# Routing rearranged, norm chain with squares from PSUM, and four modulation pairs as plain fp32 products in a two-layer decoder step

## What is computed

```python
def run_layer(x, c, s0, l):
    mod = (jax.nn.silu(c) @ w_ada[l] + b_ada[l])[:, None, :]
    sh1, sc1, g1, sh2, sc2, g2 = jnp.split(mod, 6, axis=-1)
    h = _rmsnorm(x, norm_pre_mix[l]) * (1.0 + sc1) + sh1
    mix, s_new, v_rows = _mixer(h, s0, lb[l], ...)          # gMLP and HGRN2 branches, then w_out
    x = x + g1 * _rmsnorm(mix, norm_post_mix[l])
    h = _rmsnorm(x, norm_pre_ffn[l]) * (1.0 + sc2) + sh2
    f = _swiglu(h, ...) if l % 2 == 0 else _moe(h, ...)
    return x + g2 * _rmsnorm(f, norm_post_ffn[l]), s_new, v_rows

def _moe(h, w_router, b_router, w_gate, w_up, w_down):
    logits = (h @ w_router) + b_router
    top_vals, top_idx = lax.top_k(logits, TOP_K)            # 2 of 8
    combine = ...                                           # softmax of the two, per expert
    for e in range(N_EXPERTS):
        out = out + combine[..., e:e + 1] * _swiglu(h, w_gate[e], w_up[e], w_down[e])   # 1024 -> 2816 -> 1024
```

## Time and profile before

| | before |
|---|---|
| median of 3 runs | 2442.24 us (2438.5 to 2442.84) |
| profiled execution | 2435.61 us |
| its span | 2433.8 us |
| mean granted TensorE clock | 0.958 |
| TensorE busy | 2254.9 us, 93% |
| VectorE busy | 1656.9 us, 68% |
| ScalarE busy | 1261.8 us, 52% |
| GpSimd busy | 73.6 us, 3% |

### The profile page before, as it was taken

One profiled execution on the slowest core, in us unless ns is written; L12 is line 12 of the kernel. 1 busy time (PEld: TensorE's weight loads), 2 busy tenths in 40 slices (PEclk: granted clock), 3 DMA queues, 4 the chain that ended last, 5 costly groups with the idle time before them and its releaser, 6 DMA issues.

```text
span 2433.8 us, 36240 instructions
## 1 busy us (share of the span) xinstructions
PE 2254.9 (93%) x13683; PEld 2040.0 (84%) x13683; DVE 1656.9 (68%) x1771; ACT 1261.8 (52%) x1267; POOL 73.6 (3%) x111
## 2 busy tenths in 40 slices
PE   5999999997999979999989759999999999999996
PEld 4899898986999969999989648888888888788884
DVE  5566566576555564655656368888888888888886
ACT  5433235354544444223434336766767677676764
POOL 3000000101000010000010000000000000000000
PEclk9999999998999989999989759999999999999997
DMA  8444345554566634232444209988989989898993
GB/s 266 151 126 152 104 148 156 191 178 121 177 196 191 199 112 139 83 105 96 139 147 139 104 25 328 348 331 310 343 298 359 333 321 352 297 346 320 348 334 135
DMA packets 279077, 520.13 MB, mean 214 GB/s; under 512 B 17911, under 2 KB 191049, under 8 KB 278962
## 3 DMA queue, kind: packets, MB, share of 16 engines
q1 hardware_dynamic: 270656, 493.94, 58.6%
q0 software_dynamic: 7936, 23.24, 3.0%
q10 hardware_dynamic: 370, 1.35, 0.2%
HBM read 507.19 MB, written 11.27 MB: 213 GB/s over the span
## 4 chain that ended last, share of the span: by engine, by line
PE 77%; DVE 9%; DMA 6%; issue 4%; ACT 3%; SPq 0%; DVEq 0%; ACTq 0%; POOL 0%; POOLq 0%
PE ps L1542 10%; PE ps L1543 9%; PE ps L1574 8%; PE ps L1917 5%; PE ps L1923 5%; PE ps L1918 5%; DMA mraw<-in_w_exp_up 5%; PE ps L1593 4%; PE ps L1954 4%; PE ps L1955 4%; PE ps L1960 4%; PE ps L1663 3%; PE ps L1886 2%; PE ps L1502 2%; DVE rstd L516 2%
## 5 line engine op out<-in xcount | busy, mean ns | idle before, releaser
L1015 DVE TENSOR_TENSOR mlo<-mraw,mhi 128x2048 fp32r<-128x2048 f32 (+1 forms) x319 | 691.5, 2168 | 85.1 <-ACT mhi L1340 73.8
L1340 ACT ACTIVATE mhi<-mraw 128x2048 fp32r<-128x2048 f32 (+1 forms) x320 | 582.8, 1822 | 275.0 <-DMA mraw<-in_w_exp_up 213.1
L473 DVE TENSOR_TENSOR wlo<-raw,whi 128x1024 fp32r<-128x1024 f32 x340 | 414.4, 1219 | 298.6 <-ACT whi L1102 275.9
L1542 PE MATMUL ps<-h1h,whi 128*128 128x320 f32 x1248 | 402.0, 333 | 25.5 <-DVE h1l L547 20.0
L1102 ACT ACTIVATE whi<-raw 128x1024 fp32r<-128x1024 f32 x340 | 338.8, 1046 | 108.0 <-PE ps L1599 75.1
L1543 PE MATMUL ps<-h1l,whi 128*128 128x320 f32 x1248 | 378.1, 314 | 0.0
L1917 PE MATMUL ps<-mhi,xeh 128*128 128x512 f32 (+1 forms) x864 | 327.7, 379 | 7.2 <-DVE sg L1032 4.7
L1918 PE MATMUL ps<-mhi,xel 128*128 128x512 f32 (+1 forms) x864 | 322.5, 373 | 0.0
L1542 PEld LDWEIGHTS ps<-h1h,whi 128*128 128x128 f32 x1248 | 241.4, 193 | 33.2 <-issue 29.4
L1543 PEld LDWEIGHTS ps<-h1l,whi 128*128 128x128 f32 x1248 | 241.8, 194 | 2.6 <-issue 2.6
L1923 PE MATMUL ps<-mlo,xeh 128*128 128x512 f32 (+1 forms) x864 | 225.7, 373 | 0.3 <-DVE mlo L1015 0.3
(11 more groups left out here) (327 smaller groups left out, 3175.1 us busy)
## 6 DMA issues: line engine op xcount, KB each, us to landing
mraw<-in_w_exp_down SPq DMA_DIRECT2D x198, 512.0 KB, 6.4
mraw<-in_w_exp_gate SPq DMA_DIRECT2D x154, 512.0 KB, 4.7
mraw<-in_w_exp_up SPq DMA_DIRECT2D x144, 512.0 KB, 5.9
raw<-in_w_in SPq DMA_DIRECT2D x128, 512.0 KB, 3.8
raw<-in_w_ada SPq DMA_DIRECT2D x96, 512.0 KB, 3.6
mraw<-in_w_exp_gate SPq DMA_DIRECT2D x72, 384.0 KB, 3.6
mraw<-in_w_exp_up SPq DMA_DIRECT2D x72, 384.0 KB, 4.8
raw<-in_w_ffn_gate SPq DMA_DIRECT2D x22, 512.0 KB, 5.5
```

The lines of the kernel that those rows point to most:

```text
L473: V.tensor_tensor(WLO[:, (u - 1) % RAW_UNITS, 0:w], RAW[:, u % RAW_UNITS, 0:w], WHI[:, u % HI_UNITS, 0:w].bitcast(F32), ALU.subtract).then ...
L1015: V.tensor_tensor(MLO[:, (n - 1) % RAW_RING, 0:w], MRAW[:, n % RAW_RING, 0:w], MHI[:, n % HI_RING, 0:w].bitcast(F32), ALU.subtract).then_i ...
L1340: A.activation(MHI[:, n % HI_RING, 0:w], MRAW[:, n % RAW_RING, 0:w], ACT.Copy).then_inc(m_hi, 1)
L1542: M.matmul(out_, w, v[0], start=start, stop=False, skip_group_check=True)
```

## The change

- **Start.** The sequence of pairs is scale 4 to 7, then shift 0 to 3 (FIRST_PAIRS). Units 8 to 15, which hold the four shift pairs, aren't split: TensorE multiplies `raw` with an fp32 copy of the conditioning vector (CSF, nine columns). Each pair is turned by itself one pair behind. x is normalized and scaled while the shifts are computed; the lower bounds' softmax stands behind the operands. One transfer of GpSimd (the masks) is issued later.
- **Norms.** ScalarE squares the PSUM banks, then copies. Statistics of the chunk before stand in the middle of a chunk. VectorE multiplies each chunk with the gate while the projection runs; behind the reciprocal it takes two d at a time with all 320 columns (640 elements): one product and one sum. The samples' share of the pre-norm is done in halves of four d, its first step ahead of the statistics; low parts of coming units (`lows`) stand inside the wait for them. The first chunk behind a norm goes d by d (BY_K).
- **Routing.** Two units of sample transposes and two of the prompt stand ahead of the router, two behind it. Memsets move to GpSimd. The first two expert pairs are split ahead of the router's result, the next on both engines ahead of the gathers. `choose(0)` follows the positions. Count and extra tables move into job 0, which is written out ahead of the loop, behind positions 17, 19, 21, 23, 25 and 28 (TABLE_PAIRS).
- **End.** Transposes in two halves of four d, copies shared by ScalarE and VectorE.

```diff
+HM_ORDER = [4, 5, 0, 2, 1, 3]
+TABLE_PAIRS = {17: 0, 19: 1, 21: 2, 23: 3, 25: 4, 28: 5}
...
+FIRST_PAIRS = (4, 5, 6, 7, 0, 1, 2, 3)
+DIRECT = range(8, 16)
...
+            def gate_dve(l, w, g):
+                dve.wait_ge(ada_made, (g + KD) // 2)
                 st(V.tensor_tensor(AM[:, :, :], MOD[:, g:g + KD, :],
                                    VEC[:, 1, w + 8 * l:w + 8 * l + 8].unsqueeze(2).broadcast_to([P, KD, SEQS]),
                                    ALU.mult))
+            def gated(d):
+                return see.note(V.tensor_scalar(SA[:, d, 0:TP], SA[:, d, 0:TP], AM[:, d, 0:1], None, ALU.mult), dve_step)
+            def gated_chunk(c, k):
+                dve.wait_ge(psum_out, c + 1)
+                gated(2 * k)
+                gated(2 * k + 1)
+            def post_norm_dve():
+                st(V.tensor_tensor(samples(SA), samples(SA), seq(AM), ALU.mult))
                 stats_dve(T, D, KD)
-                st(V.tensor_tensor(SA[:, :, TP:T], SA[:, :, TP:T], rb_samples, ALU.mult))
-                st(V.tensor_tensor(samples(SA), samples(SA), seq(AM), ALU.mult))
-                V.tensor_tensor(X[:, :, TP:T], X[:, :, TP:T], SA[:, :, TP:T], ALU.add)
                 made = []
-                for d in range(KD + 1):
-                    if d < KD:
-                        made.append(see.note(V.scalar_tensor_tensor(SA[:, d, 0:TP], SA[:, d, 0:TP], AM[:, d, 0:1], rb,
-                                                                    ALU.mult, ALU.mult), dve_step))
-                    if d:
-                        dve.wait_ge(dve_step, made[d - 1])
-                        see.note(V.tensor_tensor(X[:, d - 1, 0:TP], X[:, d - 1, 0:TP], SA[:, d - 1, 0:TP], ALU.add),
-                                 x_ready)
+                for q in range(5):
+                    s, p = slice(2 * q, 2 * q + 2), slice(2 * q - 2, 2 * q)
+                    if q < 4:
+                        made.append(see.note(V.tensor_tensor(SA[:, s, :], SA[:, s, :], over_k(RSTD[:, 0:T], 2),
+                                                             ALU.mult), dve_step))
+                    if q:
+                        dve.wait_ge(dve_step, made[q - 1])
+                        V.tensor_tensor(X[:, p, :], X[:, p, :], SA[:, p, :], ALU.add).then_inc(x_ready, 2)
+                        see.n[id(x_ready)] = see.n.get(id(x_ready), 0) + 2
...
+            def first_modulation(i):
+                see.next(turned)
+                modulation(FIRST_PAIRS[i], 1,
+                           PS[:, 4 + i % 2, 0:32].rearrange("p (t n) -> p t n", t=2)[:, :, 0:SEQS])
+                dve.wait_ge(ada_made, i + 1)
+            lo_until(6)
+            first_modulation(0)
+            lo_until(8)
+            first_modulation(1)
+            stats_dve(T, D, KD)
+            first_modulation(2)
+            first_modulation(3)
+            st(V.scalar_tensor_tensor(AM[:, :, :], MOD[:, KD:2 * KD, :], 1.0,
+                                      VEC[:, 1, 0:KD].unsqueeze(2).broadcast_to([P, KD, SEQS]), ALU.add, ALU.mult))
+            st(V.tensor_tensor(samples(HT), samples(X), seq(AM), ALU.mult))
+            st(V.tensor_tensor(HT[:, :, TP:T], HT[:, :, TP:T],
+                               RSTD[:, TP:T].unsqueeze(1).broadcast_to([P, KD, TS]), ALU.mult))
+            for d in range(KD):
+                see.note(V.scalar_tensor_tensor(HT[:, d, 0:TP], X[:, d, 0:TP], AM[:, d, 0:1], RSTD[:, 0:TP],
+                                                ALU.mult, ALU.mult), sem("xr_made"))
+            dve.wait_ge(sem("xr_made"), KD)
...
+            mark["hm"] = x[0]
+            def hm_low(i):
+                aux()
+                dst, src = hm_unit(HML, HM_ORDER[i], x[0] - 1)
+                see.next(sem("hm_hi"))
+                V.tensor_tensor(dst, src, hm_unit(HMH, HM_ORDER[i], 0)[0].bitcast(F32), ALU.subtract)\
+                    .then_inc(aux_out, 1)
+            for i in range(4):
+                hm_low(i)
+            st(V.memset(LG[:, :, :], 0.0))
+            m_lo_part(0, 0)
+            m_lo_part(0, 1)
...
+            choose(0)
+            m_lo_part(0, 2)
+            m_lo_part(0, 3)
+            dve.wait_ge(m_aux_out, 2)
+            V.memset(SW[:, :], 0.0).then_inc(y_made, 1)
+            def tables(part):
+                if part == 0:
+                    first_table()
+                elif part <= EXTRA:
+                    extra_table(part - 1)
+                else:
+                    st(V.tensor_copy(XF[:, 4:5], CNT[:, 5, NE - 1:NE]))
+                    V.tensor_copy(XI[0:1, 0:5], XF[0:1, 0:5]).then_inc(sem("routed"), 1)
+                    see.next(sem("routed"))
...
-            V.memset(SA[:, :, :], 0.0).then_inc(m_aux_out, 1)
-            V.memset(YEH[:, :].bitcast(F32), 0.0)
-            V.memset(PTS[:, :].bitcast(F32), 0.0)
-            V.memset(YEL[:, :].bitcast(F32), 0.0).then_inc(m_aux_out, 1)
...
+                    if first and p in TABLE_PAIRS:
+                        tables(TABLE_PAIRS[p])
+            job_dve(0, first=True)
+            with dve.Fori(1, NE) as job:
                 job_dve(job)
             dve.wait_ge(sem("routed"), 1)
...
+            def out_chunk(c, k):
+                j = k % 2
+                act.wait_ge(unit_used, ENDS[c])
+                for m in range(2):
+                    square(PS[:, 2 * j + m, 0:T])
+                A.activation(SA[:, 2 * k:2 * k + 2, :], PS[:, 2 * j:2 * j + 2, 0:T], ACT.Copy).then_inc(psum_out, 1)
+                if k == 3:
+                    root(T)
+                hi_next(c)
...
+            for i in range(4):
+                hm_high(i)
+            m_hi_part(0, 0)
+            m_hi_part(0, 1)
+            see.next(sem("top_made"))
+            A.activation(PR[:, :, 0:1], PR[:, :, 0:1], ACT.Exp).then_inc(sem("top_exp"), 1)
+            hm_high(4)
+            hm_high(5)
+            for n in range(2, HI_RING):
+                m_hi_part(0, n)
             for k in range(4):
                 gathered(k, k)
-            for n in range(HI_RING):
-                m_hi_part(0, n)
...
+            for t in (HMH[TS:P, 2, :], HML[TS:P, 2, :]):
+                see.step(pool.memset(t.bitcast(F32), 0.0), sem("hm_zero"))
+            for t in (YEH, PTS, YEL):
+                see.step(pool.memset(t[:, :].bitcast(F32), 0.0), sem("pool_step"))
+            pool.wait_ge(x_ready, 3 * KD)
+            pool.memset(SA[:, :, :], 0.0).then_inc(m_aux_out, 2)
+            pool.wait_ge(sem("y_out"), 2 * TT)
...
+            def first_rows(i):
+                if 2 * i not in DIRECT:
+                    rows(i, i % 4)
+                    return
+                for part in range(2):
+                    u = 2 * i + part
+                    pe.wait_ge(raw_in[u % RAW_UNITS], 16 * (u // RAW_UNITS + 1))
+                    for k in range(4):
+                        ins = M.matmul(PS[0:SEQS, i % 4, 0:CW], CSF[:, 4 * part + k, :],
+                                       RAW[:, u % RAW_UNITS, k * CW:(k + 1) * CW],
+                                       start=(4 * part + k == 0), stop=(4 * part + k == KD - 1))
+                    ins.then_inc(unit_used, 1)
...
+            first_rows(1)
+            pe.wait_ge(aux_out, 7)
+            pe.wait_ge(sem("sum_made"), 1)
+            first_turn(0)
+            first_rows(2)
+            first_turn(1)
             pe.wait_ge(sem("ones_set"), 1)
-            pe.wait_ge(aux_out, 7)
-            for q in range(ADA_FIRST // 2):
-                if q >= 4:
-                    pe.wait_ge(rows_out, q - 3)
-                rows(q, q % 4)
-                if q == 1:
-                    stats()
-            pe.wait_ge(rows_out, ADA_FIRST // 2)
-            pe.wait_ge(sem("sum_made"), 1)
-            turn(ROWS0, 0, ADA_FIRST)
+            for k in range(KD):
+                stat(k == 0, k == KD - 1)
+            for i in range(3, KD):
+                first_rows(i)
+                first_turn(i - 1)
+            first_turn(KD - 1)
...
+            for h in range(2):
+                pe.wait_ge(x_ready, 3 * KD + 4 * h + 4)
+                for t in range(TT):
+                    b, n, t0 = (4 + t if h else (0, 1, 3)[t]), (P if t < 2 else TS), P * t
+                    for d in range(4):
+                        ins = M.transpose(PS[0:n, b, d * P:(d + 1) * P], X[:, 4 * h + d, t0:t0 + n], ident)
+                    ins.then_inc(sem("y_in"), 1)
```

396 lines of the change are left out of this document (223 added, 173 removed).

## The result

The changed kernel took 2402.14 us (median of 4 runs, 2399.2 to 2403.36), the kernel before 2440.51 (4 runs, 2438.5 to 2442.84); the ratio is 0.9842 with a 95% interval of 0.983 to 0.9854. The forecast was 2395 with 2376 to 2415: the direction and the range held, and the gain was 38 us instead of 47. The profiled execution took 2402.61 (span 2400.8). Before, it was 2435.61, so that between the two profiled executions lie only 33.0 us.

What follows compares the result with a forecast made beforehand. TensorE, busy 93% of the span, was taken to bound the kernel, so edits pay where it waits for VectorE. Terms -15.8 - 8.7 - 26.9 + 8.3 - 4.1 = -47.2 gave median 2395 us, range 2376 to 2415.

Steps and rivals of the forecast that it cites:

- The start: Up to the second f chunk: new order and plain products bring it to 59.7 instead of 75.51, -15.8 us.
- (a): Norm gaps: squares from PSUM and statistics in mid-chunk give -1.9 us in layer 0's projection, -0.5 dense FFN, +0.3 layer 1.
- (b): Norm gaps, reciprocal to last x update: 640-element instructions take 6.2 us instead of 8.0; 1.15 seen three times, -3.4.
- (c): First chunk behind a pre-norm: less sample work ahead and d by d order, -1.6 us at each of two places.
- (d): Layer 1's mixer up to its projection's reciprocal: copy and two gate products follow the squares on VectorE, +0.3 us.
- The gap: Routing, second reciprocal to first expert product: gathers 24.8 us earlier, at +26.0; with earlier high and low parts, -26.9.
- rival B: Routing gap: clock is up when gathers begin, gathers 5.2 us instead of 10.5; 8 us more gained, 2387; chance 0.13.
- Job 0: First expert job: tables in VectorE's queue make low parts of pairs 24 to 30 late, +8.3 us.
- C: Job 0: tables are hidden by TensorE's larger backlog, the +8.3 falls, 2387 us; chance 0.14.
- F: Expert jobs: VectorE's lateness goes on past job 0, 8.3 us in all nine, 2461, slower than before; chance 0.02.
- D: Start: plain products or their chain at half clock, or pair 3 after 39; gain only 2 us, 2409; chance 0.12.
- E: Routing gap: transposes, copies and low parts alternate through two slots, router slips another 7 us, 2402; chance 0.08.

Runs made afterwards that it cites:

- second trace: The changed kernel run once more, unedited, beside the other experiments; 2400.18 us.
- e12: Changed kernel with the four shift pairs split again instead of plain products, their low parts queued ahead of the modulation of the pair before; 2405.15 us.
- e10: Changed kernel with a chunk's statistics again behind the next chunk instead of in its middle, squares still from PSUM; 2390.81 us.
- e2: Changed kernel with GpSimd waiting for the last x update ahead of all its memsets; 2400.1 us.
- e6: Changed kernel with all tables behind position 0 of job 0 and GpSimd's memsets behind the first half of layer 1's pre-norm; 2386.03 us.
- e4: Changed kernel with 21 extra unused fp32 products of 320 columns in two idle stretches of TensorE ahead of routing; 2398.31 us.
- e11: Changed kernel with 14 extra unused fp32 products of 320 columns right ahead of the gathers; 2397.69 us.
- e1: Changed kernel with all count and extra tables behind position 0 of job 0; 2383.7 us.

## Why the prediction was right, and where it was off

The terms came to 47.2 us, the two profiled executions lie 33.0 apart. The 14.2 between them, by the table: the start 4.6, the norms 6.4, the gap 0.2, job 0 1.2, the later jobs 1.9, the tail -0.1. **The offset** of 6.6 us between a profiled execution and the median was carried over and wasn't there after (2402.61 and 2402.14). That gave back 7 of the 14, so the median came out only 7 us off. This part is luck: no run shows where the offset comes from.

**The start** was right in size in the second trace, -15.1 for -15.8, and its marks fit one by one: pair 3 done at 35.7 (36.4 forecast), first f product at 53.0 (52.6), plain products 0.44 us apart (0.424). The landing of one weight unit, which I had not priced, made it -11.2 in the first trace, within the bounds of 2 to 19. Little of it belongs to the plain products: e12 shows them at 3 us or less; the rest is the new order of the work.

**The norms** were forecast at -8.7 and came to -2.3. (a) The step "it now takes the earlier pair's place: -1.9" failed. The earlier trace rows shows TensorE busy at 573.84 and idle only for the 0.61 before 575.69; work that is moved ahead on a busy engine still has to be done there. By the table of e10 layer 0's projection gained 0.84 us, 0.2 by the place of the statistics and 0.64 with the squares from PSUM, about the wait of 0.61. The row f1 to r1 can't show that, since what stands ahead of the projection in it took 462.3 to 467.0 us in traces of equal programs. In the dense FFN, for -0.5, it became 0.23 longer, and the middle of the chunk costs 1.07 there. (b) The duration of the wide updates was right, 0.82 us, and so was nearly what TensorE saw of them: its statistics begin 2.98 us behind the reciprocal instead of 3.95, at all three places and in every trace, 0.97 for the 1.15 forecast. The rows have -1.9, -0.3 and -1.25 because the sixteen records of statistics themselves took 6.22, 7.52 and 6.67 us where they had taken 7.09, 6.79 and 6.94. (c) The chunk d by d was right behind r2 (-1.6) and too high behind r4 (-0.8). (d) Layer 1's mixer became 3.2 us longer for the +0.3: 1.8 is the next point and 1.1 the statistics in the middle of the chunk. The clock has no part in it: up to the projection the mixer took 413.64 us before and 413.95 after, both of the longer value.

**The memsets** were the step with the wrong cover. "The memsets go to GpSimd, which has nothing else there" was true of GpSimd and said nothing of VectorE beside it: the gate products took 2.47 us instead of 0.70. That is 1.8 us (e2, e6). The Trainium skill, SBUF — State Buffer, section Who interferes with whom, says that VectorE and GpSimd share one pair of ports as an exclusive lock, that tensor_scalar can take it in its 2-port modes, and that whoever issues first blocks the other for its whole instruction. The trace agrees that the gate products, SBUF to SBUF, are held for whole memsets. It doesn't bear out the order: the first gate product's record starts at 1350.59, ahead of the memset's at 1350.90, and yet it is the one that ends late. By the same section an instruction with at most one SBUF input outside those modes doesn't contend; the mean, a TENSOR_SCALAR that reads PSUM, agrees, 0.49 us beside a memset as without. That it is the ports is the page's account; the runs show only who is held up.

**The gap** was right to 0.2 us: -25.0 and -1.7 for -24.8 and -2.1, with four units of transposes on the path and the half clock kept. e4 and e11 add something on rival B, which did not come. In e4 the clock was up when the second rest ended, and the gathers still ran at 0.50; whether the narrow products or the short rests of 1.38 and 2.58 us brought it down isn't shown. The Trainium skill, TensorE: Matmul & The Clock Gate, section What's actually happening, has the clock throttled by default and released by activity. e11 agrees, 0.50 behind the prefix products and 1.00 behind 28 wide records. In e4 the clock stood at 0.50 from 1375.9 to 1389 while TensorE was busy for 12.8 of these 13.1 us; no run here tells what keeps it down there.

**Job 0** was right in size, +9.5 and +8.1 for +8.3, and in place: the waits are at pairs 24 to 30. Of the 9.5 us 5.9 are waits; in the first of them the clock falls as well (0.88 from 1476 to 1490). What I had said of the cover was right, but its consequence was missed: VectorE idles at the job's beginning, where all tables fit (e1). Rivals C and F fall by the same rows: the tables weren't hidden, and the later jobs are longer by 1.9 and 4.9 us in all, not by 8 each. D falls by the plain products 0.44 us apart, E by the router at +8.9. **The tail** was right: -4.2 for -4.1 by the table's row; from the last product of the experts to the stores it is 28.98 us instead of 33.39.

## What to carry to other kernels

Side work that is taken off a critical gap has to be put where its engine idles for data, not where the code has room: the same 12 us of tables cost 7 to 10 us at one place of job 0 and nothing at another. Work moved forward on an engine that is busy is not saved, and if it comes from a place where the engine would have waited anyway, it is lost: the statistics in the middle of a chunk cost 1.07 us at two of three places. And before a memset is given to an idle GpSimd, look at what VectorE does beside it.

## What the runs showed of the hardware

- A TENSOR_SCALAR on VectorE (fp32, 256 columns from SBUF to SBUF, two in 0.61 to 0.70 us) is held up while GpSimd runs a memset: two took 2.47 us, each ending 0.15 us behind the end of a memset. The one of 320 columns from PSUM (0.49 us), TENSOR_TENSOR (0.67) and the reciprocal (2.15) take as long beside memsets as without.
- TensorE's clock fell from 2.4 to 1.2 GHz behind rests of 1.38 and 2.58 us, within 0.2 us of the first of 48 products of 8 columns (e4), and stayed there through these and 48 gathers of 128 columns, with TensorE nearly always busy; behind 14 wide fp32 products, among which the clock rose, the same gathers ran at 2.4 GHz in 5.7 us (e11).
- Equal programs differ from execution to execution by 3.9 us at the start, once with a weight unit that lands late and twice without, by 1.1 to 1.6 us in the sixteen records of statistics between r3 and r4, and by 1.4 to 3.1 us in a mixer, in steps, by where the clock falls or rises.
